# Moving one head's finish, the conv work and one branch product inside the z tiles of a decoder layer

## The reference

```python
z = x @ w_in                                   # q | forget | input | out-gate | B | C | h | gate_a | gate_b
o   = HGRN2 recurrence over 8 heads (chunks of 64)
o   = o * rsqrt(mean(o * o) + eps) * hg_norm_g * silu(og)
yc  = B * causal_depthwise_conv3(C * h, conv_w, conv_b)
mix = (sigmoid(ga) * (o @ w_branch_a) + sigmoid(gb) * (yc @ w_branch_b)) @ w_out
x   = layer_norm(ALPHA * x + mix)
x   = layer_norm(ALPHA * x + peer(x))          # top 16 of 16384 experts for each of 8 heads
x   = x + sigmoid(x @ ple_w_gate) * (p @ ple_w_proj)
```

## Time and profile before

| | us |
|---|---|
| median of 3 runs | 1886.6 |
| lowest and highest | 1884.12, 1887.56 |
| the profiled execution's own time | 1887.56 |
| its span | 1885.6 |
| TensorE busy in the span | 1604.0 (85%) |
| VectorE busy | 1295.5 (69%) |
| ScalarE busy | 755.9 (40%) |
| mean granted TensorE clock | 0.968 of full speed |

### The profile page before, as it was taken

How to read it: one execution, slowest core, us unless ns; L and a number is a source line. 1 busy time by engine, 2 the same in 40 slices (tenths; PEclk the granted TensorE clock), 3 DMA queues, 4 the chain that set the end, 5 groups by cost and what they waited for, 6 DMA issues and landing times.

```text
span 1885.6 us, 17008 instructions
## 1 busy us (share of the span) xinstructions
PE 1604.0 (85%) x5064; PEld 892.1 (47%) x5064; DVE 1295.5 (69%) x2770; ACT 755.9 (40%) x1903; POOL 488.9 (26%) x531
## 2 busy tenths in 40 slices
PE   7999999779999999688988867787878778787787
PEld 6887877665555557344434322232222223222223
DVE  4444576168997679867877887777666677766653
ACT  6566674132122211534333434434444444444432
POOL 0000000022222222223333333333333333333330
PEclk9999999889999999889999979999999999999999
DMA  5112257799999989999999999999999999999993
GB/s 205 53 67 89 89 226 278 266 373 409 398 381 407 377 318 380 372 403 399 400 386 409 414 414 414 421 396 414 422 420 421 421 398 416 421 421 421 422 418 144
DMA packets 94212, 655.37 MB, mean 348 GB/s; under 512 B 10288, under 2 KB 14128, under 8 KB 15920
## 3 DMA queue, kind: packets, MB, share of 16 engines
q0 software_dynamic: 73728, 536.90, 69.6%
q1 hardware_dynamic: 20400, 117.48, 16.3%
HBM read 652.24 MB, written 2.10 MB: 347 GB/s over the span
## 4 chain that ended last, share of the span: by engine, by line
PE 39%; DMA 34%; DVE 11%; ACT 10%; issue 5%; POOL 1%; SPq 0%; ACTq 0%; DVEq 0%; POOLq 0%
DMA uv<-in_pk_uv,idx 32%; PE psum L1554 11%; PE psum L1648 10%; PE psum L1410 4%; PE psum L1573 4%; DVE uv L1264 4%; PE psum L1587 2%; PE psum L1525 2%; PE psum L1616 2%; DVE oT L1277 2%; ACT diag L813 1%; PE psum L1506 1%; DMA raw<-in_w_in 1%; POOL uv L578 1%; ACT coef L805 1%
## 5 line engine op out<-in xcount | busy, mean ns | idle before, releaser
L1648 PE MATMUL psum<-uv,diag 128*128 128x512 f32 x1424 | 722.1, 637 | 222.8 <-ACT diag L813 219.5
L1264 DVE CUSTOM_DVE_ANT_0 uv<-uv,psum 128x1024 f32<-128x1024 f32 x512 | 622.8, 1217 | 322.2 <-DMA uv<-in_pk_uv,idx 316.0
L578 POOL DMA_INDIRECT uv<-in_pk_uv,idx x512 | 485.4, 948 | 1360.0 <-DVE oT L1277 502.0
L1648 PEld LDWEIGHTS psum<-uv,diag 128*128 128x128 f32 x1424 | 258.2, 197 | 657.9 <-ACT diag L813 447.0
L801 ACT ACTIVATE gelu<-dots 128x1 f32<-128x1 f32 x512 | 103.4, 202 | 791.7 <-DVE dots L1264 789.8
L1554 PE MATMUL psum<-xT,raw 128*128 128x384 f32 x640 | 206.6, 486 | 0.0
L1277 DVE SCALAR_TENSOR_TENSOR oT<-uv,coef,oT 128x1024 f32<-128x1024 f32 x152 | 194.4, 1279 | 13.8 <-ACT coef L805 13.8
L1554 PEld LDWEIGHTS psum<-xT,raw 128*128 128x128 f32 x640 | 121.5, 190 | 84.5
L805 ACT ACTIVATE coef<-gelu,weight 128x1 f32<-128x1 f32 x512 | 150.8, 295 | 16.6
L813 ACT ACTIVATE diag<-ident,coef 128x128 f32<-128x128 f32 x356 | 143.0, 402 | 11.6
L1410 PE MATMUL psum<-xTh,w_hi 128*128 128x512 f32 x256 | 104.9, 410 | 9.7 <-DVE xTl L991 9.7
(11 more groups left out here) (203 smaller groups left out, 1656.8 us busy)
## 6 DMA issues: line engine op xcount, KB each, us to landing
raw<-in_w_in SPq DMA_DIRECT2D x56, 1024.0 KB, 6.9
raw<-in_pk_w_q SPq DMA_DIRECT2D x16, 1024.0 KB, 8.7
raw<-in_w_branch_a SPq DMA_DIRECT2D x8, 1024.0 KB, 7.2
raw<-in_w_branch_b SPq DMA_DIRECT2D x8, 1024.0 KB, 6.8
raw<-in_w_out SPq DMA_DIRECT2D x8, 1024.0 KB, 10.0
uv<-in_pk_uv,idx POOLq DMA_INDIRECT x512, 9.9
w_gate<-in_ple_w_gate SPq DMA_DIRECT2D x1, 4096.0 KB, 16.1
x_raw<-in_x_t SPq DMA_DIRECT2D x4, 512.0 KB, 7.3
```

Of the source, the lines that this page charges most:

```text
L578: pool.indirect_dma_start(uv[:, r % UV, :], None, pk_uv, bass.IndirectOffsetOnAxis(idx[:, i % 2, j:j + 1], 0)).then_inc(row_in[r % UV], 16)
L1264: V.tensor_tensor_reduce(u, u, x_cur[:], 1.0, 0.0, ALU.mult, ALU.add, dots[:, r % 32:r % 32 + 1]).then_inc(dot_done, 1)
L1648: last = T.matmul(B[i][:], diag[:, n % DR, :], uv[:, r % UV, D + i * 512:D + (i + 1) * 512], start=(r in FIRST), stop=(k == BLOCK_ROWS - 1 ...
```

## The change

Five things move; no instruction is added or left out.

1. `rms_tail(6)` on ScalarE and `final(6)` on VectorE go from behind quarter 3 to behind quarter 1.
2. `rms_tail(7)` goes from behind quarter 23 to behind `z_out(3)`, ahead of quarter 20. `final(7)` goes from behind quarter 25 to ahead of quarter 20.
3. `conv0(0)`, `gate_conv0(0)`, `conv0(1)` and `gate_conv0(1)` go from behind the last quarter to places between quarters 19 and 36. `u_of(1)` goes from behind quarter 23 to behind quarter 21.
4. The turn of the first `u_tok` goes ahead of tile 4 on TensorE, so that `conv0(0)` has its operand.
5. `branch0(0)` goes ahead of tile 9 on TensorE. The table of uses follows.

```diff
@@ PSUM uses
+            if m == 4:
+                use(3, "ut", 0)
             if m == 5:
-                use(3, "ut", 0)
                 use(6, "cbt", 0)
...
+            if m == 9:
+                use(5, "branch0", 0)
             use(Z_BANK[m], "z", m)
-        use(5, "branch0", 0)
@@ ScalarE
-            for n in range(1, 4):
-                zh(n)
+            zh(1)
             rms_tail(HEADS - 2)
+            zh(2)
+            zh(3)
             og_sigmoid(HEADS - 1)
...
             z_out(3)
-            for n in range(20, 24):
-                zh(n)
             rms_tail(HEADS - 1)
-            for n in range(24, 28):
+            for n in range(20, 28):
                 zh(n)
@@ VectorE
-            for n in range(1, 4):
-                zl(n)
+            zl(1)
             final(HEADS - 2, 0)
+            zl(2)
+            zl(3)
             og_out(HEADS - 1, 1)
...
-            for n in range(12, 24):
+            for n in range(12, 20):
                 zl(n)
+            final(HEADS - 1, 1)
+            conv0(0)
+            zl(20)
+            zl(21)
             u_of(1)
-            zl(24)
-            zl(25)
-            final(HEADS - 1, 1)
-            for n in range(26, 40):
+            zl(22)
+            zl(23)
+            gate_conv0(0)
+            for n in range(24, 32):
                 zl(n)
-            for q in range(2):
-                conv0(q)
-                gate_conv0(q)
+            conv0(1)
+            for n in range(32, 36):
+                zl(n)
+            gate_conv0(1)
+            for n in range(36, 40):
+                zl(n)
@@ TensorE
             mean_square(HEADS - 1)
+            turn_tok(u_tok, t_reader(USE["z", 1]), "ut", 0)
             z_tile(4)
-            turn_tok(u_tok, t_reader(USE["z", 1]), "ut", 0)
...
             z_tile(8)
+            branch0(0)
             z_tile(9)
-            for n in range(4):
+            for n in range(1, 4):
                 branch0(n)
```

## The result

| | before | after |
|---|---|---|
| median, us | 1888.91 (22 runs) | 1899.46 (22 runs) |
| lowest, highest | 1884.12, 1897.91 | 1891.63, 1906.73 |
| ratio, 95% interval | | 1.0055 [1.0043, 1.0067] |
| span of the profiled execution | 1885.6 | 1896.1 |
| first indices (L1256, after L1265) | 385.2 | 392.3 |

The change makes the kernel slower by 10.4 us, 8.1 to 12.7 by the interval. The forecast had the direction and 7.45 us. The time it named was 1894.5, with 1898.5 as the upper end, and the measured median lies above it. Of the 5 us, 2.3 are the reference: the three runs known then had a median of 1886.6, twenty-two have 1888.91.

The account below looks back on a forecast made before the run. It took the prologue's load, ScalarE high-part and VectorE low-part loop feeding TensorE as the bound on the stretch changed. Early move 0, vector and branch moves +7.15, clock +0.3 gave 7.45 us: 1894.5 us, range 1889 to 1898.5.

Parts of the forecast that it names:

- The middle move: Head 7's finish and first conv block ahead of quarter 20: it starts 6.8 us late, TensorE idles 5 us before tile 5.
- The later vector move: Second conv block ahead of quarter 32: it holds VectorE from 301.4 to 305.1, so quarter 35 ends 5.65 us late.
- the branch product: First branch product ahead of tile 9: waits 2.5 us for weights, starts at 314.5; the run of three shifts +7.15 us.
- Carrying the shift one to one: After the branch products: nothing downstream has a start of its own, so the shift reaches the first gather unchanged.
- 0 us for the early move: Head 6's finish before quarters 2 and 3: new wait in tile 0 replaces the slow clock in tile 1; 0 taken.
- +0.3 us for the new waits: Lower clock after new TensorE waits before tiles 5, 8 and the first branch product; +0.3 taken, bounds 0 and +2.1.
- the upper end of +0.8 us: Tiles 0 and 1: cost of moving head 6's finish if the clock drops as before; the other end was -0.8 us.
- Rival B: New TensorE waits: one to two unabsorbed half-clock stretches of 1.7 to 2.1 us, 9.3 to 12 us total; chance 0.17.
- The bound of +2.1 us: Upper limit for lower clock after the new waits, from the slow w_out product: 15.9 us instead of 13.8.
- Rivals A: VectorE loop: half is absorbed, only one conv block lengthens it; 3.5 us, 1890; chance 0.11.
- C: VectorE's idle slots take the whole finish of head 7 and conv work: faster, up to -4.55 us, 1882; chance 0.05.
- D: Prologue: reordered work is off the path and cancels; 0 to +3 us, 1888; chance 0.07.

Follow-up runs that it names:

- single-part profiles: Kernel before with one part each: head 6's finish earlier, 1.0017; head 7's finish earlier, 0.9999; conv blocks among low parts, 1.0002; first branch product before tile 9, 1.0011.
- the pause: Kernel before with 17 chained VectorE copies ahead of the first norm, a pure delay of about 7 us; ratio 1.0037, total 7.0 us later.
- the branch move alone: Kernel before with only the first branch product put ahead of tile 9 on TensorE; ratio 1.0011 [0.9993, 1.0028].
- The fill: Changed kernel with ten extra 512-column matmuls on TensorE in its wait for the branch weights; ratio 1.0046 [1.0028, 1.0063].

## Why the prediction was right in kind and wrong in size

*The middle move* was right step by step. `final(7)` was forecast for 278 and came at 277.70, the conv block 279.4 and 279.09, quarter 20 283.05 and 282.69, TensorE's wait 5 and 4.69 us, tile 7 landed 295.6 and 295.2.

*The later vector move and the branch product* were right: `conv0(1)` from 301.4 and 300.89, the branch product at 314.5 and 314.06 with a wait of 2.5 and 2.52 us, the first `ycT` product at 333.85 and 333.40. The single-part profiles bear out that VectorE's conv work shows no cost by itself and is paid for behind the finish. The table loads ahead of `final(7)` took their 1.28 us and nothing more: ScalarE's Ln started at 275.03 behind a load that began at 273.74, and the Exp at 277.03 behind one from 275.74.

*Carrying the shift one to one* through the loop agrees with the pause, within an interval of 3.8 to 10.0 us.

*What failed is the clock, in two terms of the sum: 0 us for the early move and +0.3 us for the new waits.* "I take 0" for the early move rested on the slow stretch of tile 1 in the earlier trace rows: I set a new wait against an old one with its price. The old price was an accident of that execution. Four other profiles with that code have the first `ycT` product at 324.60 to 325.17, mean 324.9, against 326.69. Against the usual execution the early move costs 1.3 us in the prologue and not 0, and the whole change starts from a line 1.8 us lower. In 2 of 6 profiles the move's own wait was followed by the lower clock as well, 1.4 to 1.5 us more in tile 0; the upper end of +0.8 us did not hold this case, as it was again reckoned against the slow tile 1. The second term, "I take +0.3", was the clock after the new wait ahead of the branch product: it was 1.5 us in the second profile of the changed kernel (8.61 against 7.14) and 1.6 in the branch move alone, and 0 in the first. With both profiles of the changed kernel and the five that share before's code up to there the difference at the first `ycT` product is 335.0 - 325.3 = 9.8 us, and at the first indices, with two and two, 394.75 - 385.35 = 9.4. The comparisons measured 10.4 and 9.4. So the prologue accounts for the whole cost, and no part of it needs the loop. With 4.9 us between two profiles of the changed kernel this agreement is in part luck.

*Rival B* (unabsorbed slow stretches, 9.3 to 12 us, 0.17) has the number. Its mechanism is that of the second profile, with the two stretches in tile 0 and in the branch product; in the first profile of the changed kernel neither came about. The bound of +2.1 us on the clock was there, and +0.3 was too near its lower end. A bound for before's own execution was missing: nothing in the sum allowed for the profile of before being the slow one of its kind at this place. "The two slow stretches of before" were one there; the other is that of the `w_out` product in the earlier trace rows. Rivals A, C and D fell with the places of the low parts.

How much of the 10 us is clock and how much are waits on average over executions stays open. The fill could have told and did not.

## What to carry to other kernels

Work that is free in a queue's slack can stop being free when something that waits is put ahead of it: three moves that cost 1.5 us singly cost 6.2 us together, at the first `ycT` product. Before a price is read from one stretch of one profile, look whether that stretch is usual; a clock that fell after a short wait in one execution may hold in the next, on both sides of the comparison. A load issued for later work ahead of one that is wanted now is worth looking for: moving 1.5 MB behind `w_out` gained 4.2 us (0.8 to 7.6), where this reordering lost 10.4.

## What the runs showed of the hardware

TensorE's granted clock after a wait of 2.1 to 2.6 us is not a fixed outcome: for the same wait in the same program it was 1.00 in one execution and 0.65 over 4 us in another, or 1.00 and 0.53 in tile 1 of the kernel before. It fell in 1 of 8 profiles after 2.1 us, and in 4 of 10 places after 2.4 to 2.6. After waits of 1.16 and 0.69 us on both sides of the second turn of the mix it was 1.00 in one profile and 0.72 over 6 us in another. After 3.7 to 4.7 us it fell each time. Where the wait was filled with matmuls, during the norm, the next 32 passes took 3.81 us instead of 5.4 to 6.7. And the row loop, with the same instructions, varied by 18 us over fourteen profiles, more than the effect under study, so that a span alone could have shown this change as a gain: the kernel without the branch move has a span 2.3 us shorter than before and a timed ratio of 1.0022.
